# The S5 mixer's projection and core as one stage, with a real scan and tables prepared during the FFN

## The reference, cut to what matters

```python
def s5_mixer(x, w_in, lam_re, lam_im, log_dt, b_re, b_im, c_re, c_im, d_skip, w_glu):
    u = (x @ w_in).astype(f32)                     # 512 tokens, 1024 features = 64 groups of 16
    lam = lax.complex(lam_re, lam_im)              # 64 states per group
    dt = jnp.exp(log_dt)[:, None]
    a_bar = jnp.exp(lam * dt)
    b_bar = ((a_bar - 1.0) / lam)[..., None] * lax.complex(b_re, b_im)
    c = lax.complex(c_re, c_im)
    ...
    def step(h, u_c):                              # per chunk of tokens
        bu = jnp.einsum('gpc,btgc->btgp', b_bar, u_c)
        _, hs = lax.associative_scan(binop, (a_bar, bu), axis=1)
        hs = hs + a_pow[None] * h[:, None]
        y = jnp.einsum('gcp,btgp->btgc', c, hs).real
        return hs[:, -1], y
    ...
    y = ys + d_skip * u
    hid = jax.nn.gelu(y, approximate=False)
    val, gate = jnp.split(hid @ w_glu, 2, axis=-1)
    return val * jax.nn.sigmoid(gate)

def swiglu(x, w1, w3, w2):
    return (jax.nn.silu(x @ w1) * (x @ w3)) @ w2
```

## Time and profile before

| | us |
|---|---|
| median of 3 runs | 2594.35 |
| lowest and highest | 2590.91, 2595.13 |
| span of the profiled execution (its run took 2590.91) | 2590.5 |
| TensorE busy | 2477.6 (96%) |
| VectorE, ScalarE, GpSimd busy | 1739.2, 1051.9, 589.9 |
| mean granted TensorE clock | 0.991 |

### The profile page before, as it was taken

The page is one execution under the profiler, slowest core; times in us unless marked ns, Lnnn a source line. Parts: engine busy times, 40 slices in busy tenths (PEclk is TensorE's granted clock), DMA queues, the critical chain, the costliest instruction groups (busy, mean ns, idle before and its releaser), DMA issues. The chain is left out here.

```text
span 2590.5 us, 41313 instructions
## 1 busy us (share of the span) xinstructions
PE 2477.6 (96%) x15961; PEld 2036.9 (79%) x15961; DVE 1739.2 (67%) x2869; ACT 1051.9 (41%) x1561; POOL 589.9 (23%) x447
## 2 busy tenths in 40 slices
PE   8998999999999989899999999998999999999998
PEld 6788887788887768899999999886776576767566
DVE  6945656467676784576666767676687567487667
ACT  4443233321212333355555555533344443344453
POOL 2404321430230020052333432440024001024001
PEclk9999999999999999999999999999999999999999
DMA  4321002346654252267776777853221211332121
GB/s 155 98 83 35 2 3 65 124 156 237 212 182 148 76 166 84 91 219 229 254 240 224 252 236 231 271 184 125 86 74 60 76 66 57 109 94 70 33 82 65
DMA packets 259968, 339.98 MB, mean 131 GB/s; under 512 B 24928, under 2 KB 217952, under 8 KB 259232
## 3 DMA queue, kind: packets, MB, share of 16 engines
q1 hardware_dynamic: 251840, 315.52, 37.6%
q0 software_dynamic: 4512, 15.99, 1.8%
q10 hardware_dynamic: 3456, 6.29, 0.8%
HBM read 318.63 MB, written 16.52 MB: 129 GB/s over the span
## 5 line engine op out<-in xcount | busy, mean ns | idle before, releaser
L3020 PE MATMUL ps<-x_feat_r,moe_w_hi 128*128 128x384 f32 x1408 | 405.1, 361 | 0.6 <-DVE x_feat_r L3132 0.6
L2545 DVE TENSOR_TENSOR moe_w_lo<-ring,moe_w_hi 128x2048 fp32r<-128x2048 f32 x144 | 316.1, 2196 | 126.8 <-ACT moe_w_hi L2540 126.6
L3023 PE MATMUL ps<-x_feat_r,moe_w_lo 128*128 128x192 f32 x1408 | 354.0, 251 | 0.0
L2540 ACT ACTIVATE moe_w_hi<-ring 128x2048 fp32r<-128x2048 f32 x144 | 254.8, 1770 | 93.5 <-PE ps L263 76.2
L3023 PEld LDWEIGHTS ps<-x_feat_r,moe_w_lo 128*128 128x128 f32 x1408 | 269.2, 191 | 0.3
L3020 PEld LDWEIGHTS ps<-x_feat_r,moe_w_hi 128*128 128x128 f32 x1408 | 264.3, 188 | 1.7 <-issue 1.4
L267 PE MATMUL ps<-x_free_r,ring_r 128*128 128x512 f32 x496 | 195.6, 394 | 0.0
L266 PE MATMUL ps<-ring_r,x_feat_r 128*128 128x256 f32 (+2 forms) x576 | 185.1, 321 | 0.0
L263 PE MATMUL ps<-x_feat_r,ffn_w_hi 128*128 128x512 f32 x352 | 139.3, 396 | 1.2 <-DVE ffn_w_lo L2488 1.2
L267 PE MATMUL ps<-x_feat_r,ffn_w_lo 128*128 128x512 f32 x352 | 139.4, 396 | 0.0
L266 PE MATMUL ps<-x_free_r,ffn_w_hi 128*128 128x512 f32 x352 | 138.5, 393 | 0.0
(11 more groups left out here) (661 smaller groups left out, 6407.1 us busy)
## 6 DMA issues: line engine op xcount, KB each, us to landing
ring<-in_moe_w SPq DMA_DIRECT2D x120, 1024.0 KB, 5.5
ring<-in_w_in SPq DMA_DIRECT2D x32, 1024.0 KB, 5.3
ring<-in_ffn_w SPq DMA_DIRECT2D x30, 1024.0 KB, 7.4
ring<-in_ada_t SPq DMA_DIRECT2D x48, 512.0 KB, 4.3
ring<-in_gdn_w_in SPq DMA_DIRECT2D x12, 1024.0 KB, 6.0
ring<-in_moe_w SPq DMA_DIRECT2D x24, 512.0 KB, 3.8
ring<-in_s_w_glu SPq DMA_DIRECT2D x8, 1024.0 KB, 5.6
ring<-in_w_out SPq DMA_DIRECT2D x8, 1024.0 KB, 6.2
```

Source lines behind the costliest of these rows:

```text
L2540: self.prog.nc.scalar.activation(self.flat(self.hi, j % SPLITS, j), self.raw(j), ACT.Copy).then_inc(self.hi_done, 1)
L2545: self.prog.nc.vector.tensor_tensor(self.flat(self.lo, j % SPLITS, j), self.raw(j), self.flat(self.hi, j % SPLITS, j).bitcast(F32), ALU.su ...
L3020: mm = nc.tensor.matmul(out, wh[:, k, cs], both[:, k, :], start=(k == 0), stop=False)
L3023: mm = nc.tensor.matmul(out[:, 0:SLOTS], wl[:, k, cs], xg[0][:, k, :], start=False, stop=(k == KD - 1))
```

## The change: what it does

The five S5 stages before the GLU become one. Its core runs in four chunks (`SC`) of eight pairs. The feature groups are projected in the order in which the chunks need them, from eight weight tiles of 128 columns in place of four of 256. For each chunk TensorE transposes the input powers (L2093), multiplies them by the chunk's inputs (L2112), computes its lags (L2125), adds the table product (L2136) and the states' product (L2146), and turns the outputs back (L2156); these pieces are put between the projections of later feature groups. The recurrence is turned by the poles' angle, so that a real scan instruction along the free axis does it for each of real and imaginary part. The input powers are computed in the FFN beside the output powers (six more VectorE operations of 128x512 a slice), stored to DRAM by one more transfer a slice, and read by ScalarE's queue chunk by chunk into one buffer (`next_tables`). The C table comes by slices too (L1791). The skip term is added on the diagonal of the lag table; GELU reads the turned outputs from PSUM. The low halves of the output are subtracted on GpSimd for chunks 0 to 2 and on VectorE for chunk 3. Fourteen fillers follow the last outputs in place of the 18 of *s5_gelu*. The diff, cut to its core:

```diff
+            self.load_c(sp, n + 2)
+            sp.wait_ge(self.p_done, n + 1)
+            sp.dma_start(self.prog.p_dram[:, :, n * self.QUADS:(n + 1) * self.QUADS], self.p
+                         ).then_inc(self.p_stored, 16)
...
+            self.input_powers(dve, n)
...
+        dve.wait_ge(self.q_done, n + 1)
+        if n:
+            dve.wait_ge(self.p_stored, 16 * n)
+        tt(p_re, b_re, re, ALU.mult)
+        link(tt(tmp, b_im, im, ALU.mult))
+        link(tt(p_re, p_re, tmp, ALU.subtract))
+        tt(p_im, b_re, im, ALU.mult)
+        link(tt(tmp, b_im, re, ALU.mult))
+        tt(p_im, p_im, tmp, ALU.add).then_inc(self.p_done, 1)
...
+            def project(n, b=None, free=None):
+                if b is not None:
+                    turn_tables(b, 0, free)
+                proj.multiply(pe, n, range(0, 3))
+                if b is not None:
+                    turn_tables(b, 1, lambda half: pe.wait_ge(t_copied, 4 * b + half + 1))
+                proj.multiply(pe, n, range(3, KD))
+            def inputs(b):
+                pe.wait_ge(t_copied, 4 * b + 4)
+                if b:
+                    pe.wait_ge(e_read, b)
+                pe.wait_ge(u_landed[b], 2 * 16 * STEP)
...
+            def lags(b, free):
+                pe.wait_ge(wide_ready, b + 1)
+                pe.wait_ge(q_landed[b], 16)
+                for half in range(2):
+                    free(half)
...
+            def outputs(b):
+                pe.wait_ge(placed[b], 32 * STEP)
+                if b:
+                    pe.wait_ge(y_copied, 2 * b)
...
+            project(0)
+            project(1)
+            project(2, 0)
+            inputs(0)
+            project(3)
+            project(4, 1, lambda half: table_bank_free(0, half))
+            inputs(1)
+            lags(0, lambda half: table_bank_free(1, half))
+            project(5)
+            project(6, 2, lag_bank_free)
+            inputs(2)
+            lags(1, lambda half: table_bank_free(2, half))
+            project(7, 3, lambda half: lag_bank_free(2 + half))
+            outputs(0)
+            turn_back(0, lambda half: table_bank_free(3, half))
+            inputs(3)
+            lags(2, lambda half: turn_bank_free(0, half))
+            outputs(1)
+            turn_back(1, lambda half: lag_bank_free(4 + half))
+            lags(3, lambda half: turn_bank_free(1, half))
+            outputs(2)
+            turn_back(2, lambda half: lag_bank_free(6 + half))
+            outputs(3)
+            pe.wait_ge(e_read, SC)
+            keep_busy(prog, E_BANK, 4)
+            turn_back(3, lambda half: turn_bank_free(2, half))
+            keep_busy(prog, E_BANK, 10)
...
+            def next_tables(b):
+                act.wait_ge(e_ready, b)
+                act.dma_start(into[:, :, :, :].rearrange("p r q n -> p r (q n)"),
+                              prog.p_dram[:, :, chunk(b)].rearrange("p r q i c -> p r (q i c)")).then_inc(p_landed, 16)
...
+            def copy_u(n):
+                act.wait_ge(proj.product, n + 1)
+                if n >= room.U_RING:
+                    act.wait_ge(u_stored[n - room.U_RING], 16)
+                u = room.u_ring[:, n % room.U_RING]
+                nc.scalar.activation(u.rearrange("p i j -> p j i"), proj.out(n).rearrange("p (j i) -> p j i", i=STEP), ACT.Copy
+                                     ).then_inc(proj.act_copied, 1)
+                act.wait_ge(proj.act_copied, n + 1)
+                act.dma_start(prog.u_dram[IN_ORDER[n]], u.rearrange("p i j -> p (i j)")).then_inc(u_stored[n], 16)
...
+            next_tables(0)
+            load_q(0)
+            proj.split_hi(act, 0)
+            proj.split_hi(act, 1)
+            proj.split_hi(act, 2)
+            copy_u(0)
+            proj.split_hi(act, 3)
+            copy_u(1)
+            proj.split_hi(act, 4)
+            load_q(1)
+            copy_tables(0)
+            copy_u(2)
+            proj.split_hi(act, 5)
+            next_tables(1)
+            copy_u(3)
+            proj.split_hi(act, 6)
+            act.wait_ge(rot_done, 1)
+            load_q(2)
+            copy_tables(1)
+            copy_u(4)
+            proj.split_hi(act, 7)
+            next_tables(2)
+            copy_lags(0)
+            copy_u(5)
+            copy_tables(2)
+            copy_u(6)
+            next_tables(3)
+            copy_lags(1)
+            copy_tables(3)
+            copy_u(7)
+            copy_y(0)
+            load_q(3)
+            finish(0)
+            copy_lags(2)
+            copy_y(1)
+            finish(1)
+            copy_lags(3)
+            copy_y(2)
+            finish(2)
+            copy_y(3)
+            finish(3)
...
+        def split_hid(engine, queue, b):
+            for gp in range(2):
+                n = 2 * b + gp
+                f = IN_ORDER[n]
+                queue.wait_ge(hid_hi_done, n + 1)
+                m = engine.tensor_tensor(prog.x_lo[:, f, :], room.hid[:, n % room.HID_RING, :],
+                                         prog.x_hi[:, f, :].bitcast(F32), ALU.subtract)
...
+            def turn_in(b):
+                t, h = room.t, room.h[b % 2]
...
+                link(nc.vector.tensor_copy(room.decay, s5.pole[:, 0, chunk(b)].unsqueeze(2).to_broadcast([P, SQ, NJ])))
+                nc.vector.memset(room.decay[:, :, 0], 0.0)
+                if b >= 2:
+                    dve.wait_ge(y_ready, 2 * (b - 2) + 2)
+                dve.wait_ge(e_ready, b + 1)
...
+                tt(h, raw, cos.unsqueeze(1).to_broadcast(shape), ALU.mult)
+                tt(t[:, 0], raw[:, 1], sin, ALU.mult)
+                tt(t[:, 1], raw[:, 0], sin, ALU.mult).then_inc(e_read, 1)
...
+            def scan(b):
+                t, h = room.t, room.h[b % 2]
...
+                for r in range(2):
+                    m = nc.vector.tensor_tensor_scan(t[:, r].rearrange("p q j -> p (q j)"), decay,
+                                                     h[:, r].rearrange("p q j -> p (q j)"), 0.0, ALU.mult, ALU.add)
...
+            rotations()
+            proj.split_lo(dve, 3)
+            proj.split_lo(dve, 4)
+            turn_in(0)
+            proj.split_lo(dve, 5)
+            scan(0)
+            turn_out(0)
+            proj.split_lo(dve, 6)
+            turn_in(1)
+            proj.split_lo(dve, 7)
+            scan(1)
+            turn_out(1)
+            turn_in(2)
+            scan(2)
+            turn_out(2)
+            turn_in(3)
+            scan(3)
+            turn_out(3)
+            split_hid(nc.vector, dve, SC - 1)
...
+            for b in range(SC):
+                zero(b)
+                add_skip(2 * b)
+                add_skip(2 * b + 1)
+                if b + 2 < SC:
+                    widen(b + 2)
+                else:
+                    split_hid(nc.gpsimd, pool, b - 2)
+            split_hid(nc.gpsimd, pool, SC - 2)
...
+            def turn_u(n):
+                sp.wait_ge(u_stored[n], 16)
+                load_turned(sp, prog.u_dram, u_blk, IN_ORDER[n], u_landed[n // 2])
+            def place(b):
+                sp.wait_ge(zeroed, b + 1)
+                sp.wait_ge(skip_added, 2 * b + 2)
...
+            for n in range(RING):
+                next_tile(RING + n)
+                turn_u(n)
+            turn_u(4)
+            place(0)
+            turn_u(5)
+            turn_u(6)
+            place(1)
+            turn_u(7)
+            place(2)
+            place(3)
...
-    W.plan("s5_u", col_tiles(inp["s5_w_in"][0], UP_COLS))
+    W.plan("s5_u", [w_in[f] for f in IN_ORDER])
-            s5_project(prog, "s5_u", u_feat, u_blk, pw[:, 0], pw[:, 1], bbar, p_t)
-        s5_gelu(prog, u_feat, s5.d_skip)
```

More of the change, by code:

```diff
@@ L1708 @@
 PI_IN = 3.1415925
-GSTEP = 8
+SC = 4
+SQ = PAIRS // SC
+QUAD = SQ // 2
+IN_ORDER = [gp * SC + b for b in range(SC) for gp in range(2)]
+LR = 2 * GC
 def reduce_angle(nc, link, x, tmp, shift=0.0):
@@ L1886, in poles @@
         link(tt(fi, fi, den, ALU.mult))
-        dve.wait_ge(self.bc_landed, 32)
+        dve.wait_ge(self.b_landed, 16)
         rep = [P, PAIRS, GC]
@@ L2014, in s5_tables @@
[L2014 to L2028 removed]
+        at = (STEP - 1 - i) * GC
@@ new lines, in turn_bank_free, with turn_tables @@
+            def turn_bank_free(b, half):
+                pe.wait_ge(gelu_done, 4 * b + 3 + half)
+            def turn_tables(b, r, free):
+                if r == 0:
+                    pe.wait_ge(p_landed, 16 * (b + 1))
+                for half in range(2):
+                    if free:
+                        free(half)
+                    for j in range(QUAD):
+                        m = nc.tensor.transpose(ps[:, MISC_BANK + half, j * P:(j + 1) * P], into[:, r, half * QUAD + j, :], ident)
+                    m.then_inc(turned, 1)
@@ new lines, in lags @@
+            def lags(b, free):
+                pe.wait_ge(wide_ready, b + 1)
+                pe.wait_ge(q_landed[b], 16)
+                for half in range(2):
+                    free(half)
+                    for n in range(QUAD):
```

(35 more changed lines are left out.)

645 lines of the change are left out of this document (246 added, 399 removed).

## The result

The changed kernel takes 2616.28 us (median of 4 runs, 2610.68 to 2617.58) beside 2594.74 for the kernel before on the same chip: a ratio of 1.0081, 95% interval 1.0065 to 1.0096. It is slower by some 21 us. The forecast was 2587, faster; the measured time lies outside the range of 2574 to 2601.

What follows compares the result with a forecast made beforehand. It took S5 as bound by barriers, VectorE in the scan and transfers at its end, the FFN by TensorE. S5 -13.2, GLU -3.0 and FFN +9.0 gave -7.2 from the median 2594.35: 2587.1 us, range 2574 to 2601.

Steps and rivals of the forecast that it cites:

- FFN, 9.0 more: At the FFN's first half's end, TensorE idles 6.0 us for tile 15's low half, plus 3.0 of low clock.
- The two delays of 4.1: In the FFN, SyncE's wait for powers delays the adaptive block 4.1 us; six VectorE operations delay the low half 4.1 more.
- GLU, 3.0 less: At the GLU's start, fillers ending with S5's last work keep TensorE's clock up: 3.0 us less, bounds 0 and 3.
- VectorE: held: In S5, rotations take 16.6 us, eight scans 5.5 to 16.4, no wait for states; rival that VectorE binds: 0.10.
- S5, 13.2 less: The merged S5 stage takes 131.6 us against 144.8: work 105.5, waits 19.8, clock 6.0, barrier 0.3.
- Lags, 6.8: In S5, TensorE's lag instructions fall to 128 in all, at 0.053 us each: 6.8 us.
- Waits, 19.8: New TensorE waits in S5: input reloads 6.3, input powers 5.3, hand-overs and GELU's bank 5.6, last placement 2.6 us.
- powers 1.0 for 5.3: In S5, each chunk's 1 MB input powers load into one buffer: waits 0, 0 and 4.5, plus 0.8 slower landing.
- hand-overs: In S5, TensorE awaits five PSUM copies of 0.6 to 0.7 us, and GELU's bank: 5.6 us.
- (a): In S5, a chunk's inputs take 9.0 us to store and reload against 7.3 of cover; 6.3 us for four.
- Clock, 6.0: In S5, two waits are long enough to drop TensorE's clock, each worth about 3.0 us.
- the rival that ended on the other side: Transfers bind S5: each chunk's reload, powers and placement come 3 to 4 us later; 2601, chance 0.20.

Runs made afterwards that it cites:

- experiment 5: Kernel before with only the change's FFN part (input powers, their store, C table by slices), S5 left in five stages: ratio 1.0045 to the kernel before.
- [1]: Changed kernel with SyncE's wait for a slice's input powers and their store one weight tile later in the FFN: ratio 1.0047 to the kernel before.
- [9]: [7] with VectorE computing a slice's input powers behind the next weight tile's low half, not ahead of it: ratio 1.0011 to the kernel before.
- [12]: [9] with placements from two queues, chunk 1's placement earlier, low halves on VectorE, and the last ten fillers removed: 2578.54 us, ratio 0.9944 to the kernel before.
- [6]: Changed kernel with the low halves of the S5 output of all four chunks on VectorE: ratio 1.0060 to the kernel before.
- [7]: Changed kernel with later powers' store, reloads ahead of placements, transfers moved off early reloads, output powers of chunks 2 and 3 later: ratio 1.0026 to the kernel before.
- experiment 4: Changed kernel with chunk 1's output powers read at S5's start and weight tiles issued behind the first two chunks' reloads: ratio 1.0038 to the kernel before.
- 3: Changed kernel with SyncE's reload of feature group 5 ahead of the first placement, group 7's ahead of the second: ratio 1.0047 to the kernel before.
- [2]: Changed kernel with fillers in S5's transfer waits, 6 ahead of each chunk's inputs and 8 ahead of the last outputs: ratio 1.0044 to the kernel before.
- [11]: Changed kernel with half of each chunk's placements issued from GpSimd's queue and all low halves on VectorE: ratio 1.0029 to the kernel before.

## Why the prediction was wrong, by its own steps

**FFN, 9.0 more: held.** Measured 8.8. Idle 6.3 for 6.0 at the place named, `ffn_w_lo` the cause, at the second half's end 0.6. Alone the part shifts S5 by 7.8 [experiment 5]. The two delays of 4.1 are both real: SyncE's wait removed halves the stall [1], the operations' place removes the rest [9].

**GLU, 3.0 less: held, as one half of a trade.** The clock is 1.00 where it was 0.51, and from its first to its last matmul of L263 the GLU takes 91.7 for 94.4 us, 2.7 less. The sum had the fillers' 9.2 us on the path, but I counted only their gain against the stage before, and not that the last ten of them hold the barrier: ScalarE's idle time ahead of the GLU went from 1.01 to 3.66, and without them it is 1.00 [12].

**VectorE: held.** Rotations 17.0 us, scans 1.17 each, no wait for states; the low halves of GpSimd are hidden [6]. The 1 us of slack behind the rotations was about right: where the reload wait ahead is gone, TensorE waits 0.8 us for tile 3's low half [7].

**S5, 13.2 less: failed; it is 12.5 more.** Predicted 131.6, measured 157.3. Three terms carry the 25.7:

- *Lags, 6.8: measured 14.7* at the full clock (4 x 3.68), +7.9. Half as many instructions, each twice as long. In the rows 128 plus 128 instructions of a 64-row, 16-column form took 0.053 each; the 128-row, 32-column form takes 0.115. I halved the count at the old price. No row had the new form, but two bounded it: L2220 (128 rows, 64 columns) at 8.1 / 128 = 0.063 and L2036 (128 rows, 128 columns) at 7.2 / 64 = 0.112, so 8 to 14 us, both over my term. Why it came out at the dear end is not shown.
- *Waits, 19.8: measured 30.4*, +10.6. Reloads 19.1 for 6.3, last placement 5.8 for 2.6; powers 1.0 for 5.3 and hand-overs 4.5 for 5.6 the other way, which is luck for the sum: the terms for reloads and powers do not come out of their own numbers either (four times 1.7 is 6.8 before the addition for weight tiles, not 6.3, and 5.3 less 1.7 is 3.6, not 4.5). The step that failed is (a): I took each reload as 9.0 us against 7.3 of cover. The cover was right (7.4 to 8.0). The 9.0 was read from a stage that moved little besides, and holds where nothing crowds it (8.9 in experiment 4); in the changed stage it is 12.0 to 13.2, by weight tiles, `q` slices and placements in the same queue and on the same engines [3, 4]. For placement I had both ends, 0.43 and 0.62 an issue, and took the wrong one: 0.600.
- *Clock, 6.0: the rest of the stage, 13.2*, +7.2. Five waits of 4 to 6 us where I counted two; each is followed by some 3.5 us of work at twice its time. The rows agree: what ran slow took 12.8 more than at the full clock, inputs 6.8, lags 2.5 (4.57 and 5.32 for 3.68), the last outputs 2.7, and a few products behind the first wait 0.8. With the clock held in most of these places S5 falls by only 5.5 [2], since some of what TensorE wins it waits again.

So the rival that ended on the other side, transfers that bind S5, was what happened, at 0.20. Its mechanism was right, and its size for reloads too: 12.8 us more than I had, 3.2 a chunk. Over all transfers it is less, 11.7 with 3.2 more for placement and 4.3 less for powers; its price of 2601 left out the lags and most of the clock that it named. Both clues that I had weighed low bear on it: the 128 issues where 96 were, since the same bytes from two queues take 7.0 us off S5 [11], and the DMA share already at 64% in the earlier trace rows, since two transfers moved away take 4.5 off [4]. Which weighs more, single profiles don't tell. The total of S5's own loss and the FFN's is 12.5 + 8.8 - 2.7 = 18.6 of the 23.5 by which the spans differ; 1.9 more was there before the FFN, and the last 3 lie behind the GLU, where I tested nothing.

## What to carry to other kernels

A chain of store, reload and use that a barrier once covered must be priced with the transfers that will run beside it, and against the work that stands over it, chunk by chunk; four waits of 4 to 6 us for reloads and one for a placement, each with its low clock, undid what the removed barriers gave. Count the issues of each queue as work: 64 small transfers at 0.6 us are 38 us of one engine's time, and a second engine's queue takes half of them. When instructions merge, take the new form's price from a row of that form or from the nearest rows on both sides, not the old price times the new count. And ask of a filler what it holds up as well as what clock it keeps.

## What the runs showed of the hardware that I had not expected

GpSimd issues a small placement in 0.528 us, no slower than SyncE's 0.601. The last reload of a chain landed in 1.6 us with nothing large beside it [4], in 3.7 when a 0.5 MB tile and a 1.15 MB slice had been issued 1 to 2 us ahead of the chain's eight reloads, and in 4.5 with such a slice issued in their middle. A matmul of 128 rows, 32 columns and 128 moved elements costs 0.115 us at the full clock, as much as one of 128 columns (0.112) and nearly twice one of 64 (0.063). The real scan costs 1.17 us for 512 columns, between my two bounds, and was never waited for.
